# Gates of three prompt tiles: added into a zeroed HBM table by indirect transfers, in place of one-hot products on TensorE

## What is computed

```python
s1 = jnp.einsum('phd,hkd->phk', q[..., :PEER_DHALF], k1)
s2 = jnp.einsum('phd,hkd->phk', q[..., PEER_DHALF:], k2)
v1, i1 = lax.top_k(s1, PEER_TOPK)
v2, i2 = lax.top_k(s2, PEER_TOPK)
cand = (v1[..., :, None] + v2[..., None, :]).reshape(PEER_BLOCK, PEER_HEADS, PEER_TOPK * PEER_TOPK)
cidx = (i1[..., :, None] * PEER_NKEYS + i2[..., None, :]).reshape(PEER_BLOCK, PEER_HEADS, PEER_TOPK * PEER_TOPK)
sc, sel = lax.top_k(cand, PEER_TOPK)
eidx = jnp.take_along_axis(cidx, sel, axis=-1)
g = jax.nn.softmax(sc.astype(jnp.float32), axis=-1).astype(hb.dtype)
act = jax.nn.gelu(jnp.einsum('phkd,pd->phk', u[eidx], hb))
return jnp.einsum('phk,phkd->pd', g * act, v[eidx])
```

## Time and profile before

| | |
|---|---|
| median of 3 runs | 3304.05 us (3300.64 to 3308.85) |
| profiled execution, own time | 3299.75 us |
| its span in the profile | 3298.0 us |
| mean granted TensorE clock | 0.996 of full speed |
| TensorE busy | 3244.7 us, 98% |
| VectorE busy | 2310.6 us, 70% |
| ScalarE busy | 1101.0 us, 33% |
| GpSimd busy | 866.2 us, 26% |

### The profile page before, as it was taken

One profiled execution on the slowest core, in us unless ns is written; L12 is line 12 of the kernel. 1 busy time (PEld: TensorE's weight loads), 2 busy tenths in 40 slices (PEclk: granted clock), 3 DMA queues, 4 the chain that ended last, 5 costly groups with the idle time before them and its releaser, 6 DMA issues.

```text
span 3298.0 us, 70880 instructions
## 1 busy us (share of the span) xinstructions
PE 3244.7 (98%) x31390; PEld 2817.8 (85%) x31390; DVE 2310.6 (70%) x3603; ACT 1101.0 (33%) x1154; POOL 866.2 (26%) x544
## 2 busy tenths in 40 slices
PE   8999999999999999999989999999999999999998
PEld 5578888888888899999978888888888888999998
DVE  5979763565655588989855795654646547889887
ACT  4153332342434333323332433233333333233332
POOL 0000000000000587888500000000000007878882
PEclk9999999999999999999999999999999999999999
DMA  8932344363647999899722323444645489898993
GB/s 366 403 123 78 126 161 157 133 225 137 220 157 232 351 354 346 322 352 358 278 84 95 117 78 139 161 157 156 212 152 200 167 292 352 333 353 333 365 365 119
DMA packets 271537, 751.33 MB, mean 228 GB/s; under 512 B 57808, under 2 KB 203360, under 8 KB 236256
## 3 DMA queue, kind: packets, MB, share of 16 engines
q1 hardware_dynamic: 220848, 613.35, 50.4%
q0 software_dynamic: 45088, 134.39, 10.7%
q10 hardware_dynamic: 5392, 0.56, 0.1%
HBM read 615.51 MB, written 132.71 MB: 227 GB/s over the span
## 4 chain that ended last, share of the span: by engine, by line
PE 94%; DVE 4%; DMA 1%; ACT 1%; issue 0%; SPq 0%; DVEq 0%; ACTq 0%
PE PS L847 43%; PE PS L888 33%; PE PS L686 5%; PE PS L876 3%; PE PS L804 3%; PE PS L674 2%; PE PS L777 2%; PE PS L736 1%; DMA ring<-whole_w 1%; ACT ring L1096 1%; PE PS L716 0%; DVE ring L1541 0%; PE PS L817 0%; PE PS L762 0%; DVE H L1517 0%; DMA arena<-whole_w 0%
## 5 line engine op out<-in xcount | busy, mean ns | idle before, releaser
L847 PE MATMUL PS<-X,ring 128*128 128x256 f16 (+1 forms) x12288 | 1434.1, 279 | 2.4 <-ACT arena L1292 2.4
L847 PEld LDWEIGHTS PS<-X,ring 128*128 128x128 f16 x12288 | 1199.5, 98 | 221.7 <-issue 2.8
L888 PE MATMUL PS<-arena,ring 128*128 128x256 f16 (+1 forms) x12288 | 1099.5, 253 | 10.7 <-DVE arena L2017 10.7
L888 PEld LDWEIGHTS PS<-arena,ring 128*128 128x128 f16 x12288 | 1028.4, 98 | 81.9 <-issue 11.2
L1541 DVE SCALAR_TENSOR_TENSOR ring<-ring 128x4096 f16<-128x4096 f32 x148 | 654.9, 4425 | 602.6 <-ACT ring L1096 602.5
L1096 ACT ACTIVATE ring<-ring 128x4096 f16<-128x4096 f32 x148 | 535.0, 3615 | 746.2 <-PE PS L888 709.5
L1445 POOL DMA_INDIRECT ACC<-V,arena x128 | 179.8, 1405 | 2167.8 <-DMA gates_dram<-ACC 2113.7
L1450 POOL DMA_INDIRECT arena<-act_dram,arena x256 | 503.4, 1966 | 150.4 <-issue 77.4
L1320 ACT ACTIVATE H<-PS 128x544 f32<-128x544 f32 x256 | 159.6, 624 | 983.9 <-PE PS L847 983.9
L2009 DVE TENSOR_TENSOR arena<-arena 128x416 f32<-128x416 f32 x256 | 219.5, 921 | 130.8 <-PE PS L888 83.7
L1445 POOL DMA_INDIRECT H<-V,arena x128 | 178.6, 1396 | 52.9 <-issue 34.7
(11 more groups left out here) (209 smaller groups left out, 1970.9 us busy)
## 6 DMA issues: line engine op xcount, KB each, us to landing
ring<-U SPq DMA_DIRECT2D x64, 2048.0 KB, 9.5
ring<-V SPq DMA_DIRECT2D x64, 2048.0 KB, 8.6
act_dram<-H SPq DMA_DIRECT2D x64, 1088.0 KB, 5.0
gates_dram<-ACC SPq DMA_DIRECT2D x52, 1024.0 KB, 5.3
arena<-gates_dram SPq DMA_DIRECT2D x32, 1664.0 KB, 16.6
arena<-act_dram SPq DMA_DIRECT2D x64, 768.0 KB
ring<-split_w SPq DMA_DIRECT2D x17, 2048.0 KB, 9.6
arena<-whole_w SPq DMA_DIRECT2D x11, 2048.0 KB, 11.7
```

The lines of the kernel that those rows point to most:

```text
L847: mm = pe.matmul(ps_row(u)[:, COLS[half]], parts[lane][:, pu, k * 512 + j * P:k * 512 + (j + 1) * P], h16(k, half, ph), start=(k == n == 0 ...
L888: mm = pe.matmul(ps_expert(i, h)[:, c % 2, :], parts[lane][:, pv, j * D + c * P:j * D + (c + 1) * P], WT[:, grp, pw, j, (0, MID)[h]:(MID, ...
```

## The change

The gates of tiles 0, 1 and 2 are no longer made by one-hot products. GpSimd first fills the dense part of the table with zeros, in 32 transfers from a small tile of zeros (`zeros`, 104 elements repeated 16 times a partition), in layer 0 after the last rows of the conditioning, in layer 1 after the last gates of layer 0 were read. VectorE computes for each of the three tiles the place of every pick in the table (`gates_to_add`), and GpSimd then issues, for each tile, 128 indirect transfers with an add at the destination, each of which adds one gate for each of 128 tokens. The 16 transfers of one head wait until the 16 of the tile's previous head have landed; `ADD_ORDER` says which tile and head comes next. Only the sample tile keeps its one-hot products, two batches a layer, which are spilled after the zeros.

`ROUTE` and `SPAN` change: tiles 0, 1, 2 come first and take 2, 3 and 3 groups, then the sample tile with 4 and the own tile with 18. In tile 0, `candidates` and `places` stand in its first group, both picks and `normalize` in its second. The table is laid out with all tokens of one expert together, so that one group's gates are contiguous: `GB` holds one group per lane, loaded with that group's activations in `v_turn`, `next_g` is gone, and `weigh` reads it without a stride. At group 30 SyncE waits for the adds as well.

```diff
-ROUTE = (SAMPLE, OWN_TILE, 0, 1, 2)
-SPAN = {SAMPLE: 4, OWN_TILE: 5, 0: 7, 1: 7, 2: 7}
+ADDED = (0, 1, 2)
+ROUTE = ADDED + (SAMPLE, OWN_TILE)
+SPAN = {0: 2, 1: 3, 2: 3, SAMPLE: 4, OWN_TILE: 18}
+ADD_ORDER = tuple((0, h) for h in range(4)) + tuple((t, h + 4 * (1 - t)) for h in range(4) for t in (1, 0)) + \
+    tuple((t, h + 4 * (2 - t)) for h in range(4) for t in (2, 1)) + tuple((2, h) for h in range(4, HEADS))
+ZEROS = 104
...
-TILE_BATCHES = {t: (NS_ if t == SAMPLE else P - OWN if t == OWN_TILE else P) // BATCH for t in ROUTE}
+TILE_BATCHES = {t: NS_ // BATCH if t == SAMPLE else 0 for t in ROUTE}
...
-        stage = ACCF[:, 0:4096].rearrange("p (s g t e) -> p s g t e", s=2, g=BODIES, t=BATCH)
+        stage = ACCF[:, 0:4096].rearrange("p (s i t) -> p s i t", s=2, i=NKEYS)
+        ADD_W = [part(6784 + 256 * t, P) for t in ADDED]
+        ADD_I = [part(6912 + 256 * t, P, dt=U32) for t in ADDED]
+        zeros = sb("zeros", [P, ZEROS])
...
-        GB = arena[:, 4096:4096 + 2 * DENSE * 8]
+        GB = part(4096, 2, 4, DENSE)
...
-                def spill(tile, b):
-
-                    n = FIRST_BATCH[tile] + b
-                    sp.wait_ge(act_read, U_ACT[l] + GATE_AT[tile, 2 * b + 1] + 1)
-                    sp.dma_start(gates_dram[:, :, dense_at(tile, b):dense_at(tile, b) + BATCH, :],
-                                 stage[:, n % 2, :, :, :]).then_inc(g_written[n % 2], 16)
+                def spill(b):
+
+                    at = OWN_AT + b * BATCH
+                    if b == 0:
+                        sp.wait_ge(zeroed, 16 * GROUPS * (l + 1))
+                    sp.wait_ge(act_read, U_ACT[l] + GATE_AT[SAMPLE, 2 * b + 1] + 1)
+                    sp.dma_start(gates.rearrange("p (i t) -> p i t", t=DENSE)[:, :, at:at + BATCH], stage[:, b, :, :]).then_inc(
+                        g_written[b], 16)
...
-                            sp.wait_ge(g_written[s], 16 * (l + 1) * NBATCH // 2)
+                            sp.wait_ge(g_written[s], 16 * (l + 1))
+                        for t in ADDED:
+                            sp.wait_ge(gate_added[t], 16 * PICKS * (l + 1))
                         for k in range(2):
-                            if k:
-                                sp.wait_ge(g_in, 16 * (l * BODIES + k))
-                            sp.dma_start(GB[:, k * DENSE * 8:(k + 1) * DENSE * 8], view[k][:, 0:DENSE * 8]).then_inc(g_in, 16)
+                            sp.dma_start(GB[:, k, :, :].rearrange("p j t -> p (j t)"), by_group[:, k, :]).then_inc(g_in[k], 16)
...
+                        sp.dma_start(GB[:, lane, :, :].rearrange("p j t -> p (j t)"), by_group[:, group, :] if isinstance(
+                            group, int) else by_group[:, bass.ds(group, 1), :].rearrange("p o n -> p (o n)")).then_inc(g_in[lane], 16)
...
-                def take_gates(n, half):
-
-                    spilled = l * NBATCH // 2 + n // 2
-                    if half == 0 and spilled:
-                        act.wait_ge(g_written[n % 2], 16 * spilled)
+                def take_gates(b, half):
+
+                    if half == 0 and l:
+                        act.wait_ge(g_written[b], 16)
                     u = next_use()
-                    act.copy(stage[:, n % 2, :, SUB * half:SUB * (half + 1), :],
-                             ps(u, 1024).rearrange("p (t g e) -> p g t e", t=SUB, e=8)).then_inc(act_read, 1)
+                    act.copy(stage[:, b, :, SUB * half:SUB * (half + 1)],
+                             ps(u, 1024).rearrange("p (t i) -> p i t", t=SUB)).then_inc(act_read, 1)
...
+            link(pool.memset(zeros[:, :], 0.0))
+            by_element = gates_dram.rearrange("p g t (e o) -> (p g t e) o", o=1)
+            gate_rows = gates_dram.rearrange("p g t e -> p (g t e)")[:, 0:NKEYS * DENSE].rearrange(
+                "p (m r n) -> m p r n", m=GROUPS, n=ZEROS)
...
+                if l == 0:
+                    pool.wait_ge(rows_done, 2 * ADA_SLOTS)
+                else:
+                    for lane in range(2):
+                        pool.wait_ge(g_in[lane], 16 * BODIES)
+                for m in range(GROUPS):
+                    pool.dma_start(gate_rows[m], zeros[:, :].unsqueeze(1).to_broadcast([P, 4 * DENSE // ZEROS, ZEROS])).then_inc(
+                        zeroed, 16)
+                pool.wait_ge(zeroed, 16 * GROUPS * (l + 1))
+                for t, h in ADD_ORDER:
+                    if h:
+                        pool.wait_ge(gate_added[t], 16 * TOPK * (HEADS * l + h))
+                    else:
+                        pool.wait_ge(adds_found, len(ADDED) * l + t + 1)
+                    for i in range(TOPK * h, TOPK * (h + 1)):
+                        pool.indirect_dma_start(by_element, bass.IndirectOffsetOnAxis(ap=ADD_I[t][:, i:i + 1], axis=0),
+                                                ADD_W[t][:, i:i + 1], None, compute_op=ALU.add).then_inc(gate_added[t], 16)
...
+                def gates_to_add(tile):
+                    link(dve.tensor_scalar(PART_A, KEYS[:, 0, :], float(DENSE), WHICH, ALU.mult, ALU.add))
+                    link(dve.tensor_scalar(PART_A, PART_A, float((tile - OWN_TILE) * P), None, ALU.add))
+                    link(dve.scalar_tensor_tensor(out=PART_A, in0=KEYS[:, 1, :], scalar=float(BODIES * T * 8), in1=PART_A,
+                                                  op0=ALU.mult, op1=ALU.add))
+                    link(dve.tensor_copy(ADD_I[tile], PART_A))
+                    dve.tensor_scalar(ADD_W[tile], GG[:, :, :].rearrange("p h k -> p (h k)"), W_SCALE, None, ALU.mult).then_inc(
+                        adds_found, 1)
...
+                        if i == (0 if tile in (0, SAMPLE) else 1):
+                            places(index, n)
                         if i == (0 if tile == SAMPLE else 1):
-                            places(index, n)
                             link(pick(0, n))
-                        if i == (0 if tile == SAMPLE else 2):
+                        if i == {0: 1, SAMPLE: 0}.get(tile, 2):
                             pick(1, n).then_inc(keys_found, 1)
-                        if i == (1 if tile == SAMPLE else 2):
+                        if i == (1 if tile in (0, SAMPLE) else 2):
                             normalize(tile, n)
+                            if tile in ADDED:
+                                dve.wait_ge(keys_found, l * len(ROUTE) + TURN_NO[tile])
+                                dve.wait_ge(gates_ready, l * len(ROUTE) + TURN_NO[tile])
+                                gates_to_add(tile)
                         if tile == OWN_TILE and i == 2:
                             dve.wait_ge(keys_found, l * len(ROUTE) + TURN_NO[tile])
                             rows_of_picks()
                         if i == turn_group(tile):
                             dve.wait_ge(act_read, q_done + 2 * NQ + 1 + TURN_AT[tile] + 1)
                             link(dve.tensor_tensor(GS[:, 1, :], GT, GS[:, 0, :], ALU.subtract))
-                            hot(tile, 0)
-                            hot(tile, 1)
-                        if TILE_BATCHES[tile] == 8 and i == turn_group(tile) + 1:
-                            for b in range(2, 6):
-                                hot(tile, b)
-                        if TILE_BATCHES[tile] == 8 and i == turn_group(tile) + 2:
-                            for b in range(6, 8):
-                                hot(tile, b)
+                            hot(0)
+                            hot(1)
...
-                    gates = GB[:, (group // 2 % 2) * DENSE * 8:(group // 2 % 2 + 1) * DENSE * 8].rearrange("p (t e) -> p t e", e=8)
                     for j in range(4):
                         a = AB[:, grp, j, :]
-                        dve.tensor_tensor(a, a, gates[:, :, 4 * grp + j], ALU.mult).then_inc(wf_ready, 1)
+                        dve.tensor_tensor(a, a, GB[:, grp, j, :], ALU.mult).then_inc(wf_ready, 1)
```

51 lines of the change are left out of this document (16 added, 35 removed).

## The result

| | before | after |
|---|---|---|
| median of the runs, us | 3304.8 (3300.6 to 3308.9, 4 runs) | 3658.0 (3648.9 to 3685.3, 4 runs) |
| profiled execution, us | 3299.75, span 3298.0 | 3648.88, span 3647.0 |

The ratio is 1.109, with a 95% interval of 1.104 to 1.113: slower by 353 us, where 51 us of gain were forecast. It came as the first rival had it: the adds end late and stage V waits.

What follows compares the result with a forecast made beforehand. TensorE, busy 98% of the span, was taken as the bound. Gate steps removed, -88.3, stalls at group 2, +6.9, and late adds, +32, took 3299.75 to 3250 us, 3254 as a median; range 3212 to 3400.

Steps and rivals of the forecast that it cites:

- the first rival: GpSimd's queue and SyncE's wait at group 30: adds slower than gathers, stage V waits; 3408 to 3660 us; chance 0.27.
- the first line of the adds: GpSimd, stage U: 384 indirect transfers per layer at the gather's undisturbed period of 1.245 us, 478 us.
- the 651 us: GpSimd: all adds of a layer with their delays, 1.70 us an add, ending at 1054 in layer 0.
- splits and two-input passes: VectorE holding up GpSimd's transfers: 29 splits at 3.7 us each, 107 us, and other two-input passes, 30 us.
- six head waits and gaps: GpSimd: six heads of tiles 0 and 2 wait for their predecessor's landing, about 5.3 us each; 28 us.
- last issue to stage V: Last add's landing, 6 us, then SyncE's gate and activation loads, store and V slot, 21 us.
- the lateness of 16 us a layer: Ahead of stage V: adds of 651 us overshoot the free 635 us in each layer, +32 us in all.
- each microsecond past 635 costs two: Ahead of stage V: adds have 635 us free per layer; any excess delays stage V in both layers.
- the break-even at 1.76 all in: GpSimd's adds: at 676 us a layer, 1.76 us each, the gain of 81.4 us is gone.
- the stall at group 2: TensorE in stage U waits for group 2's slot, split after tile 0's early selection: 3.9 and 3.0 us, +6.9 together.
- their rival: Zero fills on GpSimd end late in layer 0, at 490, adds start 87 us late: about 3340 us; chance 0.05.
- counted at nothing: Zeroing's sharing of queues with weight loads and the store of X, slack not priced beyond 5 us: no cost.

Runs made afterwards that it cites:

- the first experiment: The changed kernel with its 768 indirect transfers writing gates over the table's contents instead of adding; measured span 3257.9 us.

## Why the prediction was wrong

**The step that failed** is the first line of the adds: 384 x 1.245 = 478 us, with the sentence "I take the lower period". The base price was taken from a gather, and adding costs GpSimd 0.58 us more on every transfer: 384 x 1.845 = 708 us, 230 more in each layer. Shown by the first experiment, which changes nothing else: 1.26 us a transfer, and 5.36 us of wait ahead of stage V instead of 215.86.

The other terms of the 651 us, in layer 0 of the changed kernel:

| term | forecast, us | measured, us | from |
|---|---|---|---|
| first add | 403.3 | 409.4 | 5.4 of it the later stage U |
| base of 384 transfers | 478 | 708 | 1.845 each |
| splits and two-input passes | 137 | 104 | busy 699.2 less 384 x 1.542 less the first call |
| first call | 2 | 3.5 | 5.00 less 1.54 |
| six head waits and gaps | 28 | 26 | idle time beyond 0.30 a transfer |
| last issue to stage V | 27 (6 + 21) | 30 | 1251.3 to 1281.7 |

The delays were 33 us too high and everything else within a few microseconds, so they made up 33 of the 230. Most of the 33 are in the short passes: the splits took 95 us (107 forecast), the other passes some 9 (30 forecast). These 33 us are also why the lateness of 16 us a layer would not have come at the price of a gather. In the last term two gate loads of 832 KB come to 7.0 us at the slot's rate, and not to the 4.4 that I had put, so my own rows gave 24 us for the 21. At 842 against 635 us free, "each microsecond past 635 costs two" gives 414 us; 424 were measured.

**The price that hid in plain sight.** Both ends of the range stood in the prediction: 1.245 and 2.14 us, with the break-even at 1.76 all in, and by the upper end 856 us and 3660. The kernel took 842 and 3658. That end was right by its number and not by its reason (VectorE's passes of stage V were in it, the add's price was not). The argument against it, "0.94 us is the same for rows of 4 KB, for single elements and for state_c's 1024 runs, so it seems a fixed price", holds for transfers that only move data, as the writes at 0.96 show. None of its rows did arithmetic. With no row of the kind and the break-even between the ends, 0.27 for the rival was too little.

**What was right.** Stage U shrank by 80.8 us in both layers (81.4 forecast: 88.3 less 6.9); the stall at group 2 was 4.0 and 3.2 us (3.9 and 3.0 forecast). The zero fills took 149 us for 32 (170 forecast) and were done before the first indices, so their rival fell. The two spills a layer cost nothing in the changed kernel. With tile 2's eight more in each layer they did, so "nothing" held only for two.

**What was left out.** Zeroing was hidden from the adds, but not from what lies ahead of stage U: "counted at nothing" was 5 us in the profiled execution and 39 us where stage U starts at 378. In the profiled one VectorE waits for the store:

```profile
243.86 0.31 DVE L1533 CAST X<-H 128x288 f16<-128x288 f32 x1 [3.02 <-DMA x_dram<-X]
...
246.67 0.73 DVE L1533 CAST X<-H 128x288 f16<-128x288 f32 x1
```

In the trace of before the same cast follows at 240.21 with no wait, and the later ones take 0.30 us; beside the seven fills from 241.54 to 249.56 five of them take 0.53 to 0.73, another 2 us.

**The two rules of the Trainium skill.** From "SBUF — State Buffer", section Who interferes with whom, the prediction took the inference that a two-input pass lets descriptor generation through, and set the gather of the earlier trace rows against it. The same section has such a pass contend with a GpSimd instruction that reads SBUF, and that I left out. Both kinds of transfer stand in the trace. The adds, whose places stand in SBUF (`ADD_I`), are held: 5.33 us for the one in the split at 803.17. The zero fills, which have no places, are not:

```profile
1875.32 8.02 POOL L1436 DMA_DIRECT2D gates_dram<-zeros  x7 [23.27 <-issue]
...
1878.04 4.43 DVE L1552 SCALAR_TENSOR_TENSOR ring<-ring 128x4096 f16<-128x4096 f32 x1 [5.16 <-ACT ring L1087]
```

Seven fills take 8.02 us, 1.15 each, with a whole split in their midst, and the group at 1913.72 takes 8.04 without one. So the rows do not speak against that section, but against carrying its inference over to indirect transfers; that it is the reading of the places which is held up fits them, but no run tests it. The section also has a one-input `tensor_scalar` in a two-port mode contend with GpSimd, and a `tensor_reduce` never: the 3.48 us beside the one-input pass agree, if its double speed is such a mode, and so does the add at 452.80, which takes 1.54 us beside a reduction of 2.29. The 2.0 us of "DMA: Bandwidth & Descriptors", section Anatomy of one DMA, lie near 1.845, but the writing transfers, from the same engine into the same table, take 1.26, so that nearness explains nothing.

## What to carry to other kernels

Where a change's sum rests on an operation that no row of the trace shows, and the break-even lies between the bounds, the lower bound is no forecast: a transfer that computes may have another price than one that moves, and times 384 that is the whole result. When a queue's new work overruns the stage that is to cover it, move part of it back: two tiles of three gave a gain of 1.8% where three lost 11%. And whatever is started early to be out of the way (fills, spills in short runs) can hold up loads and stores on the path, here by 34 us ahead of stage U and by 25 us ahead of stage V, so its place is as much a part of the change as its price.

## What the runs showed that I had not expected

- Adding costs GpSimd 0.52 us (64 elements) to 0.58 us (128) per indirect transfer over writing, nearly independent of the size.
- With the same work ahead of it, stage U of layer 0 started at 344 to 347 us in four profiles and at 378 and 379 in two; with the fills 67 us later at 340 to 344 in all five.
- In layer 0 GpSimd issues seven fills in 8.0 to 8.3 us and then stands for 24.9 to 30.1 us before the next, so 32 fills of 832 KB take 149 us.
- A one-input VectorE pass at twice the speed holds up an indirect transfer for about half as long, not for nothing; a zero fill is not held up at all by the two-input pass that holds an add for 3.8 us.
- The spill of 16384 runs of 64 bytes lands in 15 us where two are sent in a layer, and in 20.7 to 22.7 us (medians) where ten are sent in a layer, tile 2's two to a group; the 2048 runs of before took 5.3 us.
